# Alternating the gate and up matmuls between two PSUM banks in the feed-forward of a streaming encoder layer

## What is computed

```
h = x @ w_in                      # q, k, v, u
x1 = layer_norm(ALPHA * x + concat(attention, pooling) @ w_out)
ffn = (silu(x1 @ w_gate) * (x1 @ w_up)) @ w_down
y = layer_norm(ALPHA * x1 + ffn)
```

## Time and profile before

| | |
|---|---|
| times of three executions | 3241.72, 3242.06, 3246.0 us |
| median | 3242.06 us |
| profiled execution: span from its first to its last instruction | 3235.9 us |
| median less that span | 6.2 us |
| TensorE busy | 2850.3 us, 88% of the span |
| VectorE, ScalarE, GpSimd busy | 1864.3, 789.7, 551.9 us |
| matmuls of L1271 (gate and up) | 6336, 1029.5 us busy |
| matmuls of L1285 (down) | 2244, 541.7 us busy |
| mean granted TensorE clock | 0.937 |

### The profile page before, as it was taken

How to read it: one execution, slowest core, us unless ns; L and a number is a source line. 1 busy time by engine, 2 the same in 40 slices (tenths; PEclk the granted TensorE clock), 3 DMA queues, 4 the chain that set the end, 5 groups by cost and what they waited for, 6 DMA issues and landing times.

```text
span 3235.9 us, 46980 instructions
## 1 busy us (share of the span) xinstructions
PE 2850.3 (88%) x16108; PEld 2526.4 (78%) x16108; DVE 1864.3 (58%) x2575; ACT 789.7 (24%) x1461; POOL 551.9 (17%) x477
## 2 busy tenths in 40 slices
PE   5999976878878788799399999999839999999995
PEld 4999974656656566587399999999839999999994
DVE  3121366979979799333255555555545555555556
ACT  3111123434434344100211121211141211111112
POOL 1000142434434444144100000000020000000002
PEclk8999997989889999899699999999969999999997
DMA  5243126231242220364311111111031121111101
GB/s 207 99 147 110 40 113 138 63 67 42 66 98 63 56 53 21 93 188 150 108 57 57 40 40 57 39 58 39 20 125 59 39 58 39 39 44 53 39 26 54
DMA packets 226386, 234.91 MB, mean 73 GB/s; under 512 B 39703, under 2 KB 196367, under 8 KB 220094
## 3 DMA queue, kind: packets, MB, share of 16 engines
q1 hardware_dynamic: 218126, 207.68, 22.4%
q0 software_dynamic: 8112, 25.44, 2.5%
HBM read 169.18 MB, written 63.89 MB: 72 GB/s over the span
## 4 chain that ended last, share of the span: by engine, by line
PE 47%; DVE 2%; ACT 1%; DMA 1%; issue 1%; SPq 0%; POOLq 0%; POOL 0%; DVEq 0%; ACTq 0%
PE bank L1271 31%; PE bank L1285 16%; DMA out_dram<-y 0%; DVE f_stats L1451 0%; ACT x1T L1370 0%; DMA graw<-in_w_up_dram 0%; DVE acc L1444 0%; DVE y L1463 0%; ACT acc L1373 0%; DVE x1T L1469 0%; DMA acc<-x_scratch 0%; PE bank L1259 0%; DVE gw L1409 0%; DVE gw L1410 0%; ACT y L1364 0%
## 5 line engine op out<-in xcount | busy, mean ns | idle before, releaser
L1271 PE MATMUL bank<-x1T,gw 128*128 128x352 f32 (+1 forms) x6336 | 1029.5, 322 | 42.9 <-DVE x1T L1469 27.6
L1271 PEld LDWEIGHTS bank<-x1T,gw 128*128 128x128 f32 x6336 | 1015.3, 190 | 54.0 <-DVE x1T L1469 28.8
L1444 DVE TENSOR_TENSOR acc<-bank,acc 128x512 f32<-128x512 f32 x748 | 509.8, 690 | 499.7 <-PE bank L1285 499.6
L1285 PE MATMUL bank<-dw,hT 128*128 128x512 f32 x2244 | 541.7, 395 | 18.5 <-DVE acc L1444 12.8
L1285 PEld LDWEIGHTS bank<-dw,hT 128*128 128x128 f32 x2244 | 421.7, 190 | 104.0 <-DVE acc L1444 16.2
L831 PE MATMUL bank<-aT,v_st 128*64 128x128 f32 x2176 | 326.5, 292 | 95.3 <-DVE aT L914 95.3
L831 PEld LDWEIGHTS bank<-aT,v_st 128*64 128x64 f32 x2176 | 243.2, 143 | 201.4 <-DVE aT L914 143.5
L503 PE MATMUL bank<-xT,whi 128*128 128x416 f32 x1280 | 348.4, 353 | 5.6 <-DVE wlo L597 4.6
L1512 POOL TENSOR_TENSOR y<-y,f_bias 128x1024 f32<-128x1024 f32 (+1 forms) x17 | 40.0, 2355 | 1640.8 <-ACT y L1364 1640.8
L809 PE MATMUL bank<-k_st,q_st 128*128 128x512 f32 (+3 forms) x640 | 239.8, 445 | 61.3 <-DMA v_st<-out_dram 34.3
L899 DVE TENSOR_TENSOR_SCAN left<-rest,left 128x512 f32<-128x512 f32 x192 | 280.8, 1463 | 22.2 <-ACT rest L862 21.1
(11 more groups left out here) (128 smaller groups left out, 2363.3 us busy)
## 6 DMA issues: line engine op xcount, KB each, us to landing
graw<-in_w_gate_dram SPq DMA_DIRECT2D x44, 512.0 KB, 4.8
graw<-in_w_up_dram SPq DMA_DIRECT2D x44, 512.0 KB, 6.0
draw<-in_w_down_dram SPq DMA_DIRECT2D x44, 512.0 KB, 3.5
k_st<-kT_scratch SPq DMA_DIRECT2D x32, 512.0 KB, 10.8
m_mixT<-mixT_scratch SPq DMA_DIRECT2D x32, 512.0 KB, 5.2
qT_scratch<-parts SPq DMA_DIRECT2D x8, 1040.0 KB, 5.6
kT_scratch<-parts SPq DMA_DIRECT2D x8, 1040.0 KB, 5.2
mixT_scratch<-parts SPq DMA_DIRECT2D x8, 1040.0 KB, 5.1
```

The costliest lines, as they stand in the source:

```text
L1271: m = pe.matmul(bank[2 * b + g][:, 0:at.stop - at.start], gw[u][g][w][:, k, :], x1T[x][:, k, at], start=k == 0 and s == 0, stop=k == KD - ...
L1285: m = pe.matmul(bank[4 + (ND * u + d) % 4][:], hT[u][a][:, t * P:(t + 1) * P], dw[u][w][:, half * 512:half * 512 + 512], start=s == 0, sto ...
L1444: dve.tensor_tensor(s, bank[4 + (ND * u + d) % 4][0:rows, :], s, ALU.add).then_inc(summed[blk], 1)
```

## The change

The loops over `g`, `k` and `s` are nested the other way round: `k`, then `s`, then `g`. The same 48 matmuls with the same operands, banks, flags and semaphores are issued in another order.

```diff
                 b, at = (NT * u + n) % 2, cols(blk, n)
-                for g in range(2):
-                    for k in range(KD):
-                        for s, (w, x) in enumerate(((0, 0), (0, 1), (1, 0))):
+                for k in range(KD):
+                    for s, (w, x) in enumerate(((0, 0), (0, 1), (1, 0))):
+                        for g in range(2):
                             m = pe.matmul(bank[2 * b + g][:, 0:at.stop - at.start], gw[u][g][w][:, k, :],
                                           x1T[x][:, k, at], start=k == 0 and s == 0, stop=k == KD - 1 and s == 2)
                 m.then_inc(gate_up[blk], 1)
```

## The result

Twenty executions of the changed kernel have a median of 3245.12 us, twenty of before 3240.7 us. The ratio is 1.0018, with a 95% interval from 1.0009 to 1.0026: slower by 0.18%, some 5.8 us. (The two medians by themselves differ by 4.4 us; the executions of one kernel scatter over 14 to 18 us, so the size is known to a few us only.) I had forecast 3242 us and no change that could be told. The time is in my range; the direction is not what I forecast.

A forecast was written before the change was run, and what follows sets the result against it. TensorE, busy 88% of the 3235.9 us span, was taken as the bound. Bank, weights and moving operand each counted 0, leaving 3235.9 us; with 6.2 us from span to median, the forecast was 3242 us, range 3232 to 3251 us.

The forecast's parts named there:

- What bounds the kernel: Feed-forward: other engines wait for TensorE, busy 88% of the span; only the distance between matmul starts counts.
- (1): Gate matmuls in L1271: neighbours now write different PSUM banks; value 0, bounds from 82 us less to nothing.
- The 13 ns of a matmul: Part of each matmul's start-to-start distance not growing with columns; all that issue order could win, 82 us over 6336 matmuls.
- (2): L1271: 16 of 48 neighbours no longer load the same weights; value 0, upper bound 12.7 us more.
- (3): L1271: half the neighbours now stream the same activations; value 0, bounds 1.0 ns a matmul, 6.3 us either way.
- rival C: Pace shifts with operand read order, up to about 1.2 ns a matmul, 3234 to 3250 us; beyond 6.5 us: faster 0.08, slower 0.07.
- L1285 unchanged: Mark of a right forecast in the profile after: the down projection's matmul rows stay as before.
- The bound of 6.3 us: Limit either way for the moving operand's effect in L1271: 6336 matmuls at 1.0 ns each.
- The 6.2 us between span and median: Whole kernel: median time exceeds profiled span by 6.2 us, from work before the first and behind the last instruction; this stays.
- A: Same-bank turnaround: matmuls wait for the previous sums in their bank, alternation hides it; up to 82 us less; chance 0.07.
- B: Lost weight reuse slows 2112 pairs in L1271; up to 12.7 us more, 3255 us; chance 0.06.
- D: Alternation makes TensorE's clock fall; 849 us more if all L1271 ran so, a tenth is 85 us; chance 0.01.

## Why the prediction was right or wrong

What bounds the kernel: right. TensorE runs without a gap in the loops, and its pace showed in the time of the forty slices in full.

(1) Bank, value 0: right, and now shown, by the run with the banks alone. The bank change inside a group and the comparison of the earlier trace rows with the earlier trace rows had spoken for it beforehand. The 13 ns of a matmul that do not grow with its columns are not a price of the bank.

(2) Weights, value 0: right. One weight tile for all 48 changed no distance by more than 1 ns.

(3) The moving operand, value 0: this is the step that failed. I had seen that equal work runs at 159.2 and 160.2 ns with the place of its operands, gave it 1.0 ns either way, and then set it to 0, arguing under rival C that shifts partly cancel over 132 groups. They do not cancel, because there are not 132 independent draws: there are three kinds of group, each repeated to 1 ns. The term also looked at the wrong feature, that half of the neighbours stream the same tile: a repeated tile costs nothing (terms swapped; rows of 1088 columns). Going from three to six matmuls on each start residue costs 22, 38 and 27 ns a group (n = 0, 1, 2), that is 0.5, 0.8 and 0.6 ns a matmul, all of one sign. I also left out the downs ("L1285 unchanged"), whose own order does not move: behind n = 0 they take 25 ns more, behind n = 1 8 ns more, behind the 320 wide group nothing. The sum is 0.12 us a slice in block 0 and 0.14 in block 1 (22 + 38 + 22 ns for the groups, 25 + 8 + 25 for the downs), over 22 slices an estimated 5.7 us, or 0.18%: 3.7 us in the gates and 2.0 in the downs. The bound of 6.3 us held, though for the downs by luck, as it was worked out for L1271 alone; the value inside it was wrong.

The sum 3235.9 + 0 was thus short by these 5.7 us. That the two profiled spans differ by just 5.7 us too is in part chance, since executions of one kernel scatter by more. The 6.2 us between span and median was misread: in each execution whose span is on record the time is 1.6 to 1.9 us above its span, and the rest of the 6.2 is that the profiled execution was faster than the median one. It cancels in a comparison of the two kernels, but it does not stay from one profile to the next: the changed kernel's median is 3.5 us above its profiled span.

Rivals: C is what happened, on its slower side and just inside the 6.5 us at which I had called it a change; A and B are refuted; D did not occur, the clock stayed at 1.00 in the middle of the blocks. On C's mark, that groups of one `n` move one way and of another the other way, the profile differs: all three moved the same way, by unequal amounts. The mark of B, 7.7 us or more at the same clock, was met by the groups of n = 0 (7.705) though B is refuted, so it could not tell B from C.

The Trainium skill, "TensorE: Matmul & The Clock Gate", section "Back-to-back issue gap", has N / 2.4 + 2.5 ns, 149 ns for 352 columns; it gives this as the gap of an isolated matmul, which the prediction did not say, and here every matmul has a weight load of its own. No run here comes down to it: the runs of 48 give 158.3 ns (7.600 us) to 163.4 ns (7.841 us), by where the moving operand starts. Its "A second HAM failure mode: psum-queue depth-cycling" was not met: with neighbours alternating banks the clock was 1.00 and the pace the same.

What stays open is why a start at residue 32 streams faster than one at 0, and why alternating residues settle at 158.3 ns beginning with 0 and at 161.6 beginning with 32. The runs show that the sequence of starts decides; they do not show the part of the chip that makes it so. Residues are counted from where `x1T` begins, and the traces do not give that address. Nor is it shown why a start of one column is slow. Other widths than 352 and 320 were not tried.

## What to carry to other kernels

Where TensorE has no gaps, an order of issue can still cost (0.18%) or win (0.3%) a little. In this kernel it was the start of the moving operand modulo 256 bytes that did it, and neither the PSUM bank nor the weights: choose row lengths and loop orders by measured distances between starts. Read that pace over many identical groups, and when a pattern repeats to the nanosecond, do not expect its shifts to average out. To split a change like this one, move the banks and the operand order separately.

## What was not expected of the hardware

- With the moving operand fixed (at column 0 the weights too), distances between matmul starts are not equal but cycle, with 158 to 165 ns at column 0 (every six matmuls) and 155 to 162 at column 32 (every four). A single distance says little; the sum over a cycle does.
- A start off by one column (4 bytes) is the slowest seen: 7.841 us a group, 3.1% over the 7.608 of column 32.
- The pace of a group carries over into the first few matmuls of the next, of another width and another line: in before the first five distances of the downs behind n = 1 are 229 to 235 ns and the others 226 or 227, and the same 18 matmuls of `downs` took 4.079 to 4.124 us by what ran ahead of them.
